# Expert stage of a hybrid encoder layer: prompt batches in pairs, twelve raw weight slots, inner rows turned behind the pair

## The reference, cut to what matters

```python
aff = softmax(ht @ w_router)                 # T x 16, per request group
gate_vals, idx = top_k(aff.T, cap)           # cap = 2*T/16: 128 sample rows, 32 prompt rows
xe  = ht[idx]
hid = silu(xe @ w_e_gate[e]) * (xe @ w_e_up[e])      # 1024 -> 2048
ye  = (hid @ w_e_down[e]) * gate_vals                # 2048 -> 1024
out = zeros(T, D).at[idx].add(ye)
```

## Time and profile before

| | |
|---|---|
| median of three runs | 3148.11 us |
| the profiled execution's own time | 3148.47 us |
| its span in the trace | 3146.9 us |
| TensorE busy, share of the span | 3011.5 us, 96% |
| VectorE busy | 1718.3 us, 55% |
| ScalarE busy | 1522.6 us, 48% |
| GpSimd busy | 567.8 us, 18% |
| mean DMA rate over the span | 191 GB/s |

### The profile page before, as it was taken

How to read it: one execution, slowest core, us unless ns; L and a number is a source line. 1 busy time by engine, 2 the same in 40 slices (tenths; PEclk the granted TensorE clock), 3 DMA queues, 4 the chain that set the end, 5 groups by cost and what they waited for, 6 DMA issues and landing times. The chain is left out here.

```text
span 3146.9 us, 51612 instructions
## 1 busy us (share of the span) xinstructions
PE 3011.5 (96%) x19346; PEld 2391.5 (76%) x19346; DVE 1718.3 (55%) x1759; ACT 1522.6 (48%) x1665; POOL 567.8 (18%) x729
## 2 busy tenths in 40 slices
PE   8999999999989999999949999999999999999998
PEld 6888887777778799878837777777777777777776
DVE  4101000555543599924267667666666666666665
ACT  4211111556632366623435665665666665556654
POOL 0038884112220000011100111000111100111100
PEclk9999999999999999999979999999999999999999
DMA  5323322333334100064447877778888777788874
GB/s 177 113 96 137 124 86 83 124 117 117 95 130 177 61 14 20 8 226 139 158 163 271 289 283 283 275 280 295 294 293 294 273 272 293 285 290 292 294 275 142
DMA packets 195566, 600.71 MB, mean 191 GB/s; under 512 B 14176, under 2 KB 44912, under 8 KB 195488
## 3 DMA queue, kind: packets, MB, share of 16 engines
q1 hardware_dynamic: 165312, 508.49, 44.2%
q0 software_dynamic: 21312, 73.35, 7.9%
q10 hardware_dynamic: 8864, 17.83, 1.6%
HBM read 522.19 MB, written 77.33 MB: 191 GB/s over the span
## 5 line engine op out<-in xcount | busy, mean ns | idle before, releaser
L2093 DVE TENSOR_TENSOR ex_w_lo<-ex_w_raw,ex_w_hi 128x2048 fp32r<-128x2048 f32 x384 | 879.9, 2292 | 450.5 <-ACT ex_w_hi L2048 450.5
L2048 ACT ACTIVATE ex_w_hi<-ex_w_raw 128x2048 fp32r<-128x2048 f32 x381 | 730.0, 1916 | 469.7 <-PE ex_ps_s L2180 469.5
L2180 PE MATMUL ex_ps_s<-ex_w_hi,ex_xS 128*128 128x512 f32 x2048 | 578.6, 396 | 0.0
L2180 PEld LDWEIGHTS ex_ps_s<-ex_w_hi,ex_xS 128*128 128x128 f32 x2048 | 376.2, 188 | 99.1 <-issue 26.3
L2180 PE MATMUL ex_ps_s<-ex_w_lo,ex_xS 128*128 128x512 f32 x1024 | 316.8, 391 | 0.0
L2180 PE MATMUL ex_ps_s<-ex_w_hi,ex_hidS 128*128 128x512 f32 x1024 | 308.1, 403 | 0.0
L2034 POOL DMA_INDIRECT y<-ex_ye_s,ex_rows_y x16 | 43.6, 2728 | 1146.4 <-DVE ex_ye_s L2136 1146.4
L2191 PE MATMUL ex_ps_p<-ex_w_raw,ex_xP 128*32 128x256 f32 x4096 | 235.3, 382 | 0.0
L109 PE MATMUL pj_ps_tok<-pj_w_hi,act_hl 128*128 128x512 f32 x560 | 223.2, 398 | 2.4 <-DVE act_hl L442 2.4
L2180 PEld LDWEIGHTS ex_ps_s<-ex_w_lo,ex_xS 128*128 128x128 f32 x1024 | 192.4, 188 | 41.2
L110 PE MATMUL pj_ps_tok<-pj_w_lo,act_hl 128*128 128x512 f32 x560 | 222.1, 397 | 0.0
(11 more groups left out here) (337 smaller groups left out, 5142.9 us busy)
## 6 DMA issues: line engine op xcount, KB each, us to landing
ex_w_raw<-w_e_gate SPq DMA_DIRECT2D x128, 1024.0 KB, 10.2
ex_w_raw<-w_e_up SPq DMA_DIRECT2D x128, 1024.0 KB, 10.4
ex_w_raw<-w_e_down SPq DMA_DIRECT2D x128, 1024.0 KB, 8.2
proj_t<-pj_stage SPq DMA_DIRECT2D x60, 256.0 KB, 2.0
pj_w_raw<-w_cols ACTq DMA_DIRECT2D x7, 2048.0 KB, 9.3
z_w_raw<-w_z SPq DMA_DIRECT2D x16, 512.0 KB, 3.9
gate_logits<-gl_z_stage SPq DMA_DIRECT2D x32, 256.0 KB, 2.1
pj_w_raw<-x SPq DMA_DIRECT2D x10, 512.0 KB, 3.9
```

Source lines behind the costliest of these rows:

```text
L2048: act.activation(whl[0][:, j % NHL], raw[:, j % NRAW], ACT.Copy).then_inc(w_hi, 1)
L2093: dve.tensor_tensor(whl[1][:, j % NHL], raw[:, j % NRAW], whl[0][:, j % NHL].bitcast(F32), ALU.subtract).then_inc(w_lo, 1)
L2180: mm = pe.matmul(ps_s[:, s, c:c + 512], x(part, k), whl[w][:, j % NHL, kk, c:c + 512], start=k == 0 and part + w == 0, stop=k == 2 * PU - ...
```

## The change

TensorE issues the prompt batches of phases f and f+1 one behind the other, ahead of the eight sample units of both, three times per expert. The raw slots become 12. The sample's eight transposes of inner rows stand directly behind the pair of batches (at j = 8 and j = 16, ahead of the sample unit) and no longer behind units 9, 10, 17 and 18. The prompt's two stand behind units 4 and 12. To make room in SBUF, silu writes straight into the hidden tile and the product is made in place; the sample's hidden and result tiles lie in one tile, `late`, which holds the choice's tiles before. SyncE's and VectorE's waits move with it. The core of the diff (left out: the repeated renamings and the start order of the loads, which takes phases 0, 1 and 2):

```diff
-        NRAW, NHL, LEAD = 8, 4, 3
+        NRAW, NHL, LEAD = 12, 4, 3
+        P_TURN, S_TURN = (4, 12), (8, 16)
@@
-        sgS, sgP = ph.sb("silu_s", [CS, HF]), ph.sb("silu_p", [P, QW])
-        hS, hP = ph.sb("hidden_s", [CS, HF]), ph.sb("hidden_p", [P, QW])
-        yS, yP = ph.sb("ye_s", [CS, D]), ph.sb("ye_p", [P, QW])
+        hS, yS = late[:, 0:HF], late[:, HF:HF + D]
+        hP, yP = ph.sb("hidden_p", [P, QW]), ph.sb("ye_p", [P, QW])
@@ SyncE
-                        sp.wait_ge(p_full, CR + PHASES * e + f - 1)
+                        sp.wait_ge(p_full, CR + PHASES * e + f - NRAW // PU + 1)
@@ ScalarE
-                        for f, at in ((0, 10), (1, 18)):
-                            for r in range(2):
-                                if j == at + r:
-                                    turn_high(e, 3 * f + r + 1, ...)
...
+                                act.wait_ge(turned, CR + XT + TURNS * e + (1 if f == 2 else 4 - TURNS))
+                                act.activation(hP[:], ps_p[:, 0, 0:QW], ACT.Silu).then_inc(act_p, 1)
...
+                        if j in S_TURN:
+                            g = S_TURN.index(j)
+                            for r in range(2):
+                                turn_high(e, 3 * g + r + 1, ...)
...
+                                act.wait_ge(turned, CR + XT + TURNS * e + (3 if f == 2 else 6 - TURNS))
+                                act.activation(hS, ps_s[:, 0], ACT.Silu).then_inc(act_s, 1)
@@ VectorE
-                        if f % 2 == 1 and j % PU == 0:
-                            dve.wait_ge(p_full, CR + PHASES * e + f + 1)
+                        if j % (2 * PU) == 2:
+                            dve.wait_ge(p_full, CR + PHASES * e + f + 2)
...
-                                dve.tensor_tensor(hS[:], sgS[:], ps_s[:, 1], ALU.mult).then_inc(dve_s, 1)
+                                dve.tensor_tensor(hS, hS, ps_s[:, 1], ALU.mult).then_inc(dve_s, 1)
@@ TensorE
-                        if i == 0:
-                            pe.wait_ge((act_p, dve_p)[f % 2], CR + 3 * e + f // 2)
+                        if i == 0 and f % 2 == 0:
                             if f == 0:
                                 pe.wait_ge(turn_out, CR + q - 2)
-                            if f >= 4:
-                                pe.wait_ge(turn_out, CR + q + 3 * (f - 4) + 1)
...
+                            if f == 4:
+                                pe.wait_ge(turn_out, CR + q + 4)
+                            for b, evacuated in enumerate((act_p, dve_p)):
+                                pe.wait_ge(evacuated, CR + 3 * e + f // 2)
+                                if f == 4:
+                                    prompt(e, f + b, lambda k, c: hidP[:, b, k % 2, CP * (k // 2):CP * (k // 2) + CP])
+                                else:
+                                    prompt(e, f + b, lambda k, c: xP[:, k])
+                        if j in S_TURN:
+                            g = S_TURN.index(j)
+                            pe.wait_ge(dve_s, CR + 3 * e + g + 1)
+                            for r in (1, 2):
+                                pe.wait_ge(turn_out, CR + q + 3 * g + r - 1)
+                                turn_hidden(g, r)
...
-                        for g, at in ((0, 8), (1, 16)):
-                            if at <= j < at + 3:
...
+                        if j in P_TURN:
+                            g = P_TURN.index(j)
+                            pe.wait_ge(dve_p, CR + 3 * e + g + 1)
+                            pe.wait_ge(turn_out, CR + q + 3 * g - 1 if g else CR + q)
+                            turn_hidden(g, 0)
@@ program
+            late = router.enter_context(nc.sbuf_tensor("choice_then_rows", [P, T + TS // 2 + 5 * CS], F32))
+            affT, vals = late[0:NE, 0:T], late[0:ROWS, T:at_lists]
```

More of the change, by code:

```diff
@@ L1933, in choose, with experts @@
         ph.clear()
-def experts(nc, affT, vals, lists, idx, h2, y, w_gate, w_up, w_down, slots_i, slots_g, slots_q, cst):
+def experts(nc, late, affT, vals, lists, idx, h2, y, w_gate, w_up, w_down, slots_i, slots_g, slots_q, cst):
     with ExitStack() as ctx:
@@ L1970, in start_weights @@
                 f, k = j // PU, slice(2 * (j % PU), 2 * (j % PU) + 2)
[L1971 removed]
+                sp.dma_start(raw[:, j], gu_d[f % 2][:, 0:1, k, f // 2 * HF:(f // 2 + 1) * HF].rearrange("p e k c -> p (e k) c")).then_inc(w_in[j], 16)
         def first_high(act):
@@ L2032, in body @@
                     ph.settle(pool)
-                    for j, (dst, src) in enumerate(((y, yS), (y_q, yP))):
-                        pool.indirect_dma_start(dst, bass.IndirectOffsetOnAxis(ap=rows_y[j][:, 0:1], axis=0), src[:], None,
+                    for j, (dst, src) in enumerate(((y, yS), (y_q, yP[:]))):
+                        pool.indirect_dma_start(dst, bass.IndirectOffsetOnAxis(ap=rows_y[j][:, 0:1], axis=0), src, None,
                                                 compute_op=ALU.add).then_inc(scattered[j], 16)
@@ L2070, in body @@
                             if f < 4:
-                                act.activation(sgP[:], ps_p[:, 0, 0:QW], ACT.Silu).then_inc(act_p, 1)
+                                act.wait_ge(turned, CR + XT + TURNS * e + (1 if f == 2 else 4 - TURNS))
+                                act.activation(hP[:], ps_p[:, 0, 0:QW], ACT.Silu).then_inc(act_p, 1)
                             else:
@@ L2074, in body @@
                                 act.activation(yP[:], ps_p[:, 0, 0:QW], ACT.Copy, scale=gate[1][:]).then_inc(act_p, 1)
+                        if j in S_TURN:
+                            g = S_TURN.index(j)
+                            for r in range(2):
+                                turn_high(e, 3 * g + r + 1, hidS[:, 0, g * FC + 4 * r:g * FC + 4 * r + 4], (3 * g + r + 1) % 2)
                         if f % 2 == 0 and j % PU == PU - 1:
@@ L2078, in body @@
                             if f < 4:
-                                act.activation(sgS[:], ps_s[:, 0], ACT.Silu).then_inc(act_s, 1)
+                                act.wait_ge(turned, CR + XT + TURNS * e + (3 if f == 2 else 6 - TURNS))
+                                act.activation(hS, ps_s[:, 0], ACT.Silu).then_inc(act_s, 1)
                             else:
-                                act.activation(yS[:], ps_s[:, 0], ACT.Copy, scale=gate[0][:]).then_inc(act_s, 1)
+                                act.activation(yS, ps_s[:, 0], ACT.Copy, scale=gate[0][:]).then_inc(act_s, 1)
                 for r in range(2):
@@ L2104, in body @@
                             low(e, j + LEAD)
-                        for f, at in ((0, 9), (1, 17)):
-                            if j == at:
+                        for f, at in enumerate(S_TURN):
+                            if j == P_TURN[f] + 1:
                                 dve.wait_ge(turned, CR + q + 3 * f + 1)
@@ L2109, in body @@
                             for r in range(2):
-                                if j == at + 1 + r:
+                                if j == at:
                                     k = slice(f * FC + 4 * r, f * FC + 4 * r + 4)
@@ L2119, in body @@
                         f = j // PU
-                        if f % 2 == 1 and j % PU == 0:
-                            dve.wait_ge(p_full, CR + PHASES * e + f + 1)
+                        if j % (2 * PU) == 2:
+                            dve.wait_ge(p_full, CR + PHASES * e + f + 2)
                             dve.wait_ge(act_p, CR + 3 * e + f // 2 + 1)
                             if f < 4:
-                                dve.wait_ge(turned, CR + q + f // 2)
-                                dve.tensor_tensor(hP[:], sgP[:], ps_p[:, 1, 0:QW], ALU.mult).then_inc(dve_p, 1)
+                                dve.tensor_tensor(hP[:], hP[:], ps_p[:, 1, 0:QW], ALU.mult).then_inc(dve_p, 1)
                             else:
@@ L2132, in body @@
                             if f < 4:
-                                dve.wait_ge(turned, CR + q + 3 * (f // 2))
-                                dve.tensor_tensor(hS[:], sgS[:], ps_s[:, 1], ALU.mult).then_inc(dve_s, 1)
+                                dve.tensor_tensor(hS, hS, ps_s[:, 1], ALU.mult).then_inc(dve_s, 1)
                             else:
-                                dve.scalar_tensor_tensor(out=yS[:], in0=ps_s[:, 1], scalar=gate[0][:], in1=yS[:],
+                                dve.scalar_tensor_tensor(out=yS, in0=ps_s[:, 1], scalar=gate[0][:], in1=yS,
                                                          op0=ALU.mult, op1=ALU.add).then_inc(dve_s, 1)
@@ L2198, in body @@
                         f, i = j // PU, j % PU
-                        if i == 0:
-                            pe.wait_ge((act_p, dve_p)[f % 2], CR + 3 * e + f // 2)
+                        if i == 0 and f % 2 == 0:
                             if f == 0:
                                 pe.wait_ge(turn_out, CR + q - 2)
-                            if f >= 4:
```

(14 more changed lines are left out.)

8 lines of the change are left out of this document (removed).

## The result

The changed kernel takes 3130.26 us (median of six runs, 3126.55 to 3131.04), beside 3147.89 us of the kernel before. The ratio is 0.9942, interval 0.9931 to 0.9952. It is 17.6 us faster by the medians, where 14.7 was forecast (3133.4, range 3126 to 3143), and the interval lies clear of 1.

The account below looks back on a forecast made before the run. The prediction took TensorE, busy 96% of the span, to bound the kernel. Its terms gave 3148.5 - 17.2 - 2.0 + 4.5 = 3133.8 us, or 3133.4 us with the runs' median 0.4 lower; range 3126 to 3143 us.

Parts of the forecast that it names:

- What bounds the kernel: Expert stage: TensorE is busy throughout and waits for nothing, so only time it spends between its instructions can be saved.
- The price of a change, 0.36 us, 48 times 17.2 us: Sample to prompt tiles and back on TensorE: pairing removes 48 changes at 0.36 us, saving 17.2 us.
- The upper bound: Second batch of a pair: it saves all of the 0.36 us, 17.2 us in the range 10.6 to 17.2.
- rival 2: Between two batches part of the price stays, and the transposes pay a second exposed load: 3145 us; chance 9%.
- Transposes, 0.06 us per place, 2.0 us: Sample's transposes moved behind the pair: 0.06 us saved at each of 32 places, 2 us; bounds -6.4 to +3.2 us.
- Do the inner rows come in time?: Behind the pair: VectorE's product is ready 2.8 us into 6.9 us, 4.1 us left; one batch alone leaves 0.8 us.
- Loads: Weight loads for the pairs: the slowest four take 17.5 us, wanted after 29 us, so 11 us in hand.
- The start, +4.5 us: First gathers: twelve loads run beside them and delay their landing, which TensorE waits for; 0 to 5.0 us, 4.5 taken.
- Rival 1: At the start, gathers share the DMA engines evenly with the loads, costing 1.6 us: 3130.5 us; chance 18%.
- Rivals 3 and 4: In pairs: second batch waits for weights, 3181 us at 1 us each, 5%; TensorE's clock falls to 1.2 GHz, 3465 us, 1%.

Follow-up runs that it names:

- E2: The changed kernel with its pairs undone: single prompt batches ahead of each phase, the sample's transposes still directly behind the batch, twelve slots kept; 3147.76 us, ratio 1.0001.
- F4: The kernel before with prompt batches replaced by plain float32 matmuls of 128*128 tiles, the prompt's product left out; 3117.54 us, ratio 0.9906.
- E5: The changed kernel with the sample's transposes between units again, one unit earlier than in E1: behind units 8, 9, 16 and 17; 3133.76 us, ratio 0.9956.
- E3: The changed kernel with pairs undone and the sample's transposes between units again, twelve slots and in-place silu kept; 3151.45 us, ratio 1.0013.
- E1: The changed kernel with pairs kept but the sample's transposes between units again, behind units 9, 10, 17 and 18; 3189.01 us, ratio 1.0132.
- F1: The changed kernel with eight loads in the choice and the other four only when the first gather has landed; 3128.13 us, ratio 0.9938.
- E4: The changed kernel itself measured again, on the chip of E1 to E3; 3129.44 us, ratio 0.9944.

## Why the prediction was right, point by point

*What bounds the kernel.* Right. TensorE was full, nothing was waited for, and the gain lay in the distances between its instructions.

*The price of a change, 0.36 us, 48 times 17.2 us.* Right. E2 against the changed kernel gives 0.36 us each and 17.3 us in the traces (18.3 by the medians). The upper bound was the right one to take: the second batch joins without a gap, so rival 2 did not come about. F4 shows that it is the change of tile shape, and hardly that of element type, that costs.

*Transposes, 0.06 us per place, 2.0 us.* The direction was right, the term was half of what it is: 0.12 us in both later periods of E5, and 0.12 in E2 against E3, 3.8 us in all. Over the plain phase of 14.69 us, eight transposes behind a batch cost 0.86 us (E2), as forecast, the first of them only 0.06 us over its pace. Between units they cost 0.98 us (E3), where I had read 0.90: my sum for a set of four ended at the third sample matmul behind it, and the next seven still start 0.231 us apart (2064.53 to 2066.15 in the kernel before) and not 0.227.

*Do the inner rows come in time?* Right for the product: ready at 2.8 us in a pair of 7.0. E2 bears out even the 0.8 us of a single batch. But the cover that I gave to the second batch was not needed for it, and the step took direct turning for a small gain of its own. It missed what pairing takes away at unit 20. Without direct turning the pairs lose 2.3 us in each expert, and in 12 of 16 the clock's 1.6 us with it (E1). Turning earlier, at either place (E5 or the changed kernel), is what lets the pairs pay. That the forecast did not fail on this is luck: the change held the remedy for a wait that the prediction did not see.

*Loads.* Right: no wait for weights, at any of 48 pairs. E3 shows that the twelve slots give nothing by themselves. Whether the pairs need all twelve no run shows.

*The start, +4.5 us.* Right in kind and 0.9 too much: 3.6 us, with F1 as the proof of the cause. The loads' end was also read too late, at 1644.7: the DMA share was 1.02 up to 1643 and 0.37 in the microsecond behind it. Rival 1, an even share of the DMA engines, gave 1.6 us, and the time measured lies next to its 3130.5 us; but its mechanism explains at most the 0.7 us by which the packets are spread wider. The other 2.6 us pass before the gather's first packet, and what holds it back is open. The Trainium skill, "DMA: Bandwidth & Descriptors", Queues, rings and completion order, has each DMA engine go round the queues packet by packet; the trace shows that this alone does not give the 3.6 us. The first transpose came at 1653.5 and not at 1655.5: 0.9 us of that is this term, the rest the earlier start of this profile.

*Not forecast:* where the clock rises in the first pair. It cost 0.5 us more than before in this profile and 0.6 less in E4's (29.76 us), so it is spread and no term of the change. The terms as measured, -17.3 - 3.8 + 3.6 = -17.5 us, stand beside -17.6 of the medians. The forecast of 14.7 us was 2.9 us short; the transposes account for 1.8 of that and the start for 0.9.

*Rivals 3 and 4.* Neither came about. The clock stayed at 1.00 through pairs of 7 us, from 1659.5 us until the last expert's matmuls were over. Inside the experts it fell only in E1, behind an idle engine and not behind a batch.

## What to carry to other kernels

When an engine is busy all the time, compare the distance of its starts within a group with the distance across groups. A change of tile shape shows there and as idle time of the weight loads, but not as idle time or as a wait of the matmuls, and equal shapes put together save it. Before an instruction group is moved, ask not only what it waits for but what it covers at the place that it leaves: a cover of 2 us in each expert was worth 56 us here with the clock's falls, over three times what the pairs save in changes of shape. And what is loaded earlier runs beside something: here a small gather that everything waited for.

## What the runs showed of the hardware

Behind a wait of TensorE of only 2.0 us (2.4 us between two starts), in an engine otherwise full, the granted clock fell from 1.00 to 0.50 in 12 of 16 cases in E1, at 1.6 us each; in the other four the same wait left it at 1.00. Which of the waits does it is not settled by these runs. A change between 128*128 and 128*32 tiles and back costs 0.32 us, told by a batch of the same length and pace in 128*128 tiles (F4); the change of element type costs 0.04 us at most. With twelve loads of 1 MB queued, a gather's first packet started 4.3 us behind its issue, and 1.7 us where eight loads had ended before it.
